# The even stage one half of the tokens at a time, and its narrow unit as one product of 448 columns

## The reference, cut to what matters

```
x = layer_norm(ALPHA * x + ffn, ln_ffn_g[layer], ln_ffn_b[layer])     # end of the first block
...
def modulate(x, shift, scale):
    return layer_norm_2(x) * (1 + scale[..., None, :]) + shift[..., None, :]
...
EVEN_IN_SIZES = (GLA_QK_W, GLA_QK_W, GLA_V_W, 2 * GLA_GATE_RANK, GLA_V_W,
                 MLA_Q_RANK, MLA_KV_RANK, MLA_ROPE, MLA_V_W)
proj = lambda h: split_cols(jnp.einsum('bnd,de->bne', h, w_in), EVEN_IN_SIZES)
gq_l, gk_l, gv_l, glr_l, gg_l, cq_l, ckv_l, kr_l, mg_l = proj(h_lat)
```

## Time and profile before

| | us |
|---|---|
| median of 3 runs (lowest, highest) | 1438.95 (1438.36, 1439.72) |
| the profiled execution | 1438.28 |
| its span, first to last instruction | 1437.0 |
| PE busy | 1109.3 (77%) |
| DVE busy | 465.4 (32%) |
| ACT busy | 323.1 (22%) |
| POOL busy | 87.9 (6%) |

### The profile page before, as it was taken

The page is one execution under the profiler, slowest core; times in us unless marked ns, Lnnn a source line. Parts: engine busy times, 40 slices in busy tenths (PEclk is TensorE's granted clock), DMA queues, the critical chain, the costliest instruction groups (busy, mean ns, idle before and its releaser), DMA issues.

```text
span 1437.0 us, 19484 instructions
## 1 busy us (share of the span) xinstructions
PE 1109.3 (77%) x8553; PEld 629.3 (44%) x8553; DVE 465.4 (32%) x943; ACT 323.1 (22%) x618; POOL 87.9 (6%) x116
## 2 busy tenths in 40 slices
PE   8999756698485656999985656666655799989998
PEld 7656312264131211897731211112111289744997
DVE  5636203101110100777720100100100077566774
ACT  4512110000310000374210000000000046433640
POOL 2311100000000000040120000000000000000100
PEclk9999978889788878999997888878787899999999
DMA  9949999999999999848999999999999964213720
GB/s 375 400 176 352 423 428 427 427 428 426 427 426 429 427 427 422 374 164 352 413 393 426 428 429 426 429 429 426 426 428 428 422 276 154 70 63 140 303 104 30
DMA packets 42699, 501.27 MB, mean 349 GB/s; under 512 B 6398, under 2 KB 7892, under 8 KB 13432
## 3 DMA queue, kind: packets, MB, share of 16 engines
q1 hardware_dynamic: 37440, 492.78, 82.0%
q10 hardware_dynamic: 3112, 5.96, 1.2%
q0 software_dynamic: 2064, 1.30, 0.3%
HBM read 498.92 MB, written 1.10 MB: 348 GB/s over the span
## 4 chain that ended last, share of the span: by engine, by line
DMA 44%; PE 39%; DVE 8%; ACT 5%; SPq 2%; issue 1%; POOL 1%; DVEq 0%; ACTq 0%; POOLq 0%
DMA weight_ring<-in_moe_w_gate_up 29%; DMA weight_ring<-in_u_down 11%; PE bank L1410 6%; PE bank L369 5%; PE bank L1440 3%; PE bank L370 3%; PE bank L372 3%; PE bank L371 3%; DMA weight_ring<-in_u_ctx_kv 2%; PE bank L632 2%; SPq L555 2%; DMA weight_ring<-in_u_last 2%; PE bank L1059 1%; PE bank L1853 1%; DVE weight_ring_rounded L410 1%
## 5 line engine op out<-in xcount | busy, mean ns | idle before, releaser
L1410 PE MATMUL bank<-weight_ring,expert_tokens 128*32 128x512 f32 x1952 | 290.7, 729 | 170.1 <-DMA weight_ring<-in_moe_w_gate_up 165.1
L1410 PEld LDWEIGHTS bank<-weight_ring,expert_tokens 128*32 128x32 f32 x1952 | 62.4, 122 | 371.3 <-DMA weight_ring<-in_moe_w_gate_up 211.0
L1440 PE MATMUL bank<-weight_ring,actT 128*32 128x256 f32 x1760 | 140.7, 478 | 60.0 <-DMA weight_ring<-in_u_down 51.7
L1644 DVE TENSOR_TENSOR act<-silu,bank 128x256 f32<-128x256 f32 x32 | 13.5, 420 | 399.1 <-ACT silu L1759 399.1
L1440 PEld LDWEIGHTS bank<-weight_ring,actT 128*32 128x32 f32 x1760 | 65.1, 132 | 126.5 <-DMA weight_ring<-in_u_down 55.6
L1759 ACT ACTIVATE silu<-bank 128x256 f32<-128x256 f32 x32 | 12.3, 384 | 452.4 <-PE bank L1410 452.4
L1658 DVE COPY expert_outs<-bank 32x256 f32<-32x256 f32 x60 | 25.1, 418 | 230.6 <-PE bank L1440 229.6
L410 DVE TENSOR_TENSOR weight_ring_rounded<-weight_ring,weight_ring_rounded 128x1024 fp32r<-128x1024 f32 (+1 forms) x76 | 89.3, 1235 | 14.3 <-ACT weight_ring_rounded L394 14.1
L394 ACT CAST weight_ring_rounded<-weight_ring 128x1024 fp32r<-128x1024 f32 (+1 forms) x72 | 70.0, 1046 | 19.5 <-DMA weight_ring<-in_u_qkv 8.8
L1776 ACT COPY expert_outs<-bank 32x256 f32<-32x256 f32 x60 | 21.9, 365 | 209.5 <-PE bank L1440 208.8
L524 POOL TENSOR_TENSOR norm_rstd<-norm_var,minus_half 128x1 f32<-128x1 f32 x12 | 12.1, 1008 | 844.2 <-DVE norm_var L1693 647.6
(11 more groups left out here) (523 smaller groups left out, 1849.7 us busy)
## 6 DMA issues: line engine op xcount, KB each, us to landing
weight_ring<-in_moe_w_gate_up SPq DMA_DIRECT2D x122, 2048.0 KB, 36.6
weight_ring<-in_u_down SPq DMA_DIRECT2D x55, 2048.0 KB, 37.1
weight_ring<-in_u_ada SPq DMA_DIRECT2D x9, 2048.0 KB, 7.8
weight_spare<-in_moe_w_gate_up SPq DMA_DIRECT2D x6, 2048.0 KB, 40.0
weight_spare<-in_u_down SPq DMA_DIRECT2D x5, 2048.0 KB, 41.1
weight_ring<-in_u_last SPq DMA_DIRECT2D x16, 512.0 KB, 32.6
...
```

Source lines behind the costliest of these rows:

```text
L1410: last = pe.matmul(up[CAP * j:CAP * (j + 1), :], B.xs[:, t, e * CAP:(e + 1) * CAP], w[:, t % 2, :, j, :], start=(t == 0), stop=(t == T - 1))
L1440: last = pe.matmul(K[3][CAP * q:CAP * (q + 1), 0:QC], B.actT[i][:, s, j * CAP:(j + 1) * CAP], w[:, jj, s, q, :], start=(j == 0 and s == 0) ...
```

## The change

Half 0 goes first. VectorE takes half 0's second moments right behind x of half 0, ahead of the norm of half 1 (second_moments_vector, called in experts_norm_vector), and hands the negated mean over; ScalarE only computes the result (first_flat_scalar). TensorE turns half 0, does 4 idle products, multiplies half 0's HIGH pass, turns half 1, and goes on with the passes of both halves. ScalarE modulates all 8 tiles of half 0, and tiles 4 to 7 of half 1, VectorE tiles 0 to 3 of half 1, each of 128 tokens. The narrow unit becomes two products of 448 columns with tokens in the partitions, n0 and n1, in one bank each. The low-rank rows then have tokens in the partitions too, so they are copied (low_rank_rows), turned by TensorE between the two column blocks of q, and copied again by ScalarE (job "lr", behind the first step of the latent attention) before the gate products. Banks keep their numbers for q and what follows. ScalarE rounds all four pieces of the narrow weights ahead of flat of half 0.

The diff, cut to its core:

```
--- before.py
+++ after.py
@@ -1712,6 +1712,8 @@
             x = B.x[:, half, :]
             v.scalar_tensor_tensor(x, x, B.rstd[:, half:half + 1], B.bias, ALU.mult, ALU.add).then_inc(*sig.tell("normed", ("x", stage, half)))
+            if half == 0 and stage == "moe1":
+                self.second_moments_vector("even", 0)
...
-    def modulated_tensor(self, stage, banks, between, block=None):
-        sig, pe, B = self.sig, self.pe, self.B
-        for c in range(2):
-            pe.wait_ge(*sig.after("summed", BEFORE[stage], 1, c))
-        for half in range(H):
...
-            pe.wait_ge(*sig.after("flat", stage, half))
-            for pair in range(T // 2):
-                for t in (2 * pair, 2 * pair + 1):
-                    o = (t % 2) * S + half * P
-                    last = pe.transpose(banks[pair][:, o:o + P], B.flat[:, half, t::T], B.ident)
-                if half == 1:
-                    last.then_inc(*sig.tell("tensor_turned", ("flat_turned", stage, pair)))
...
-    def modulated_vector(self, stage, banks, slot, hi, lo):
...
-        for pair in (0, 2):
-            v.wait_ge(*sig.after("flat_turned", stage, pair))
-            for t in (2 * pair, 2 * pair + 1):
-                v.tensor_scalar(lo[:, t, :], banks[pair][:, (t % 2) * S:(t % 2 + 1) * S], B.mod[:, slot, 1, t:t + 1],
-                                B.mod[:, slot, 0, t:t + 1], ALU.mult, ALU.add).then_inc(*sig.tell("modulated", ("modulated", stage, pair)))
-        for pair in range(T // 2):
-            both = slice(2 * pair, 2 * pair + 2)
-            v.wait_ge(*sig.after("h_rounded", stage, pair))
-            v.tensor_tensor(self.B.h_lo[stage][:, both, :], lo[:, both, :], hi[:, both, :], ALU.subtract).then_inc(
-                *sig.tell("h_split", ("features", stage, pair)))
...
-    def token_pass_tensor(self, stage, name, w, h, parts, half, bank):
+    def token_pass_tensor(self, stage, name, w, h, parts, half, bank, end=TOKENS_REST):
...
+    def second_moments_vector(self, stage, half):
+
+        sig, v, B = self.sig, self.v, self.B
+        stats, mv = (B.first_stats, B.first_mv) if half == 0 else (B.flat_stats, B.flat_mv)
+        v.wait_ge(*sig.after("x", BEFORE[stage], half))
+        for c in range(2):
+            v.bn_stats(stats[:, 6 * c:6 * c + 6], B.x[:, half, c * 512:(c + 1) * 512]).then_inc(*sig.tell("flat_moments"))
+        v.wait_ge(*sig.now("flat_moments"))
+        v.bn_aggr(mv, stats).then_inc(*sig.tell("flat_moments", ("flat_mean", stage, half)))
+        v.wait_ge(*sig.after("flat_mean", stage, half))
+        v.tensor_scalar(B.flat_var[:, half:half + 1], mv[:, 1:2], EPS_SECOND, None, ALU.add).then_inc(
+            *sig.tell("flat_variance", ("flat_variance", stage, half)))
+        if half == 0:
+            v.tensor_scalar(B.flat_sum[:, 0:1], mv[:, 0:1], -1.0, None, ALU.mult).then_inc(*sig.tell("flat_moments", ("flat_minus_mean", stage)))
...
+    def first_flat_scalar(self, stage):
+
+        sig, a, B = self.sig, self.a, self.B
+        minus_mean, bias = B.flat_sum[:, 0:1], B.flat_sum[:, 1:2]
+        a.wait_ge(*sig.after("flat_deviation", stage, 0))
+        a.wait_ge(*sig.after("flat_minus_mean", stage))
+        a.activation(bias, minus_mean, ACT.Copy, scale=B.flat_rstd[:, 0:1]).then_inc(*sig.tell("flat_steps"))
+        a.wait_ge(*sig.now("flat_steps"))
+        a.activation(B.flat[:, 0, :], B.x[:, 0, :], ACT.Identity, scale=B.flat_rstd[:, 0:1], bias=bias).then_inc(
+            *sig.tell("flat_steps", ("flat", stage, 0)))
...
-    def modulated_scalar(self, stage, banks, slot, hi, lo):
...
     EVEN_ORDER = {
...
-        "vector": ("cq", "ckr", "A", "+v", "L", "q", "A", "A", "+gg", "L", "L", "L", "v", "A", "A", "L", "+mg", "A", "A", "A"),
+        "vector": ("n1", "A", "+v", "L", "q", "A", "A", "+gg", "L", "L", "L", "v", "A", "A", "L", "+mg", "A", "A", "A"),
...
-    EVEN_JOBS = ("lr", "cq0", "cq1", "ckr0", "ckr1", "q", "k", "v0", "v1", "gg0", "gg2", "mg0", "mg2")
-    EVEN_BESIDE = ("gate0", "gate2", "lat", "cqT", "qr0", "qr1", "qrT0", "qrT1")
+    EVEN_BANKS = {"n0": 4, "n1": 5, "q": 3, "k": 4, "v0": 5, "v1": 0, "gg0": 1, "gg2": 2, "mg0": 3, "mg2": 4}
+    EVEN_AFTER = {"q": ("modulated", "even", 0, 1), "k": ("even_taken", "n0"), "v0": ("even_taken", "n1"), "v1": ("modulated", "even", 1, 0),
+                  "gg0": ("modulated", "even", 1, 1), "gg2": ("modulated", "even", 0, 0), "mg0": ("even_taken", "q"),
+                  "mg2": ("even_taken", "k")}
+    EVEN_BESIDE = ("lr", "gate0", "gate2", "lat", "cqT", "qr0", "qr1", "qrT0", "qrT1")
...
-        self.modulated_tensor("even", K, 0)
-        self.idle_products_tensor(K[5], 3)
...
+            if job == "q":
+                self.feature_pair("even", name, w, [c], h, self.even_bank(job))
+                self.low_rank_turned_tensor()
+                last = self.feature_pair("even", name, w, [c + P], h, self.even_bank(job)[:, S:2 * S])
+            else:
+                last = self.feature_pair("even", name, w, [c, c + P], h, self.even_bank(job))
...
+        banks = [self.even_bank(f"n{half}")[:, 0:w[0].shape[-1]] for half in range(H)]
+        run = lambda parts, half: self.token_pass_tensor("even", "even_narrow", w, h, parts, half, banks[half], self.WEIGHTS_REST)
+        self.halves_turned_tensor("even", 0)
+        self.idle_products_tensor(self.B.bank[5], 4)
+        run(self.HIGH, 0)
+        self.halves_turned_tensor("even", 1)
+        run(self.TOKENS_REST, 0)
+        run(self.HIGH, 1)
+        run(self.TOKENS_REST, 1)
+        for half in range(H):
+            run(self.WEIGHTS_REST, half).then_inc(
+                *sig.tell("projected", ("even", f"n{half}"), ("free", "even_narrow"), ("free", "even_narrow_hi")))
+
+    def low_rank_turned_tensor(self):
+
+        sig, pe, B = self.sig, self.pe, self.B
+        self.beside_free("lr")
+        for half in range(H):
+            pe.wait_ge(*sig.after("even_taken", f"lr{half}"))
+            last = pe.transpose(self.beside_bank("lr")[0:2 * GR, half * P:(half + 1) * P], B.lr_rows[:, half, :], B.ident)
+        last.then_inc(*sig.tell("side_products", ("beside", "lr")))
 
     def even_out(self):
...
+            buf, at = {"lr": (B.lr_rows, 0), "cq": (B.cq, 2 * GR), "ck": (B.ckr, 2 * GR + QR)}[job[0:2]]
+            dst = buf[:, int(job[-1]), :]
+            return dst, self.even_bank(f"n{job[-1]}")[:, at:at + dst.shape[-1]]
...
-        self.modulated_vector("even", K, 0, B.h_hi["even"], B.h_raw["even"])
+        self.second_norm_vector("even")
+        v.wait_ge(*sig.after("modulation", 0))
+        for q in range(2):
+            self.half_rest_vector("even", 0, q)
+        self.half_modulated_vector("even", 0, 1, range(4))
+        for q in range(2):
+            self.half_rest_vector("even", 1, q)
         self.split_weights_vector("even_narrow", T * sum(n for _, n in EVEN_W[0][1]))
         self.split_weights_vector("even_qk")
 
         def run(job):
-            for j in {"cq": ("cq1",), "ckr": ("ckr1",), "q": ("q",), "v": ("v1",)}.get(job, ()):
+            if job == "n1":
+                v.wait_ge(*sig.after("even", "n1"))
+                for j in ("lr1", "cq1", "ckr1"):
+                    v.tensor_copy(*self.even_take(j)).then_inc(*sig.tell("vector_moved", ("even_taken", j), ("even_taken", "n1")))
+                return
+            for j in {"q": ("q",), "v": ("v1",)}.get(job, ()):
...
-        self.split_weights_scalar("even_narrow", narrow, (0, 1))
-        self.flat_scalar("even")
-        self.split_weights_scalar("even_narrow", narrow, (2, 3))
-        self.modulated_scalar("even", K, 0, B.h_hi["even"], B.h_raw["even"])
+        self.split_weights_scalar("even_narrow", narrow)
+        self.first_flat_scalar("even")
+        a.wait_ge(*sig.after("modulation", 0))
+        for q in range(2):
+            self.half_modulated_scalar("even", 0, 0, range(4 * q, 4 * q + 4))
+            self.half_rounded_scalar("even", 0, q)
+        self.half_modulated_scalar("even", 0, 1, range(4, T))
+        for q in range(2):
+            self.half_rounded_scalar("even", 1, q)
...
+            if job == "n0":
+                a.wait_ge(*sig.after("even", "n0"))
+                for j in ("lr0", "cq0", "ckr0"):
+                    a.copy(*self.even_take(j)).then_inc(*sig.tell("scalar_moved", ("even_taken", j), ("even_taken", "n0")))
+                return
+            if job == "lr":
+                a.wait_ge(*sig.after("beside", "lr"))
+                a.copy(B.lrT[0:2 * GR, :], self.beside_bank("lr")[0:2 * GR, 0:S]).then_inc(*sig.tell("scalar_moved", ("beside_taken", "lr")))
+                return
...
-            pe.wait_ge(*sig.after("even_taken", "lr"))
+            pe.wait_ge(*sig.after("beside_taken", "lr"))
```

81 lines of the change are left out of this document (10 added, 71 removed), and 4 rows, old and new, of the table EVEN_ORDER.

## The result

The changed kernel takes 1441.17 us (median of 22 runs, 1439.39 to 1443.37); the kernel before, beside it, 1438.68 (22 runs, 1438.12 to 1440.05). The ratio is 1.0016, with a 95% interval of 1.001 to 1.0023: 2.5 us slower, within the 0.2% that the prediction called the same, 0.9 above its 1440.3 and inside its range. The profiled execution took 1441.83 us, its span 1440.3, against 1438.28 and 1437.0.

The account below looks back on a forecast made before the run. VectorE's queue was taken to bound the kernel through its copy of ckr: later splits and extra copies add 1.39 us, about 1.4 on the 1438.95 median, giving 1440.3 us; 8-in-10 range 1437.8 to 1442.8.

Parts of the forecast that it names:

- rival D: Narrow stage: TensorE's clock falls to 0.50 at about 1175, 4.2 us reach the path, 1444.5 us; chance 0.10.
- A: The forecast itself: VectorE's splits become the bound, 1440.3 us, own range 1439.2 to 1441.4; chance 0.69.
- The bound: Narrow stage: VectorE runs splits and three copies without a gap; TensorE's last narrow product ends 2 us before the copies.
- The start: First even transposes: flat half 0 ready at about 1165.4, but 40 idle products leave only 0.26 of 1.2 us.
- Half 0 to the second transposes: Even stage, timed from the odd stage: 5.14 + 1.01 - 0.11 us, so half 1's transposes start at 1172.5.
- The splits: VectorE's 8 weight pieces queue behind the last subtractions: start 1176.86 against 1173.12, end 3.74 us later at 1185.50.
- The sum: VectorE's copy of ckr starts at 1185.95 against 1184.56, +1.39 us, and all that follows is displaced by it.
- a small clock loss: Allowance for TensorE's clock within the 8-in-10 range, 1437.8 to 1442.8 us; no size of its own given.
- TensorE's head start is worth nothing: From 1184.56 to 1228 the moment of VectorE's ckr copy sets the time, so TensorE being ahead gains nothing.
- B: Even-stage modulations cost less than in the odd stage, by the page's figure 1.5 us less: 1438.8 us; chance 0.07.
- C: Narrow products saved come off in full, the splits not being waited for: 4.6 us less, 1434.4 us; chance 0.06.
- The covers: Half 1's moments (1.8 us later), the low-rank detour (5 us of cover) and the mla load would cost nothing.

Follow-up runs that it names:

- e3: The changed kernel with VectorE's four narrow splits moved into its idle gaps among the even stage's rests and modulations; 1438.3 us, ratio 0.9997.
- e6: e5 with 34 instead of 40 idle products ahead of the even transposes; 1439.36 us, ratio 1.0004.
- e5: The changed kernel with idle products in TensorE's narrow-stage gaps and ahead of the mg products; 1439.82 us, ratio 1.0004.
- e4: The change's 448-column products alone, both halves normed, turned and modulated together as in the kernel before; 1436.49 us, ratio 0.9986.
- e1: The changed kernel with idle products in TensorE's gaps of the narrow stage only; 1440.38 us, ratio 1.0011.
- e2: The changed kernel with 12 idle products ahead of the mg products only; 1439.81 us, ratio 1.001.
- r1: The changed kernel profiled again without any edit; 1442.21 us (one run).
- r2: The changed kernel profiled once more without any edit; 1440.57 us (one run).
- e10: e5 with each 448-column product cut into one of 288 and one of 160 columns; 1439.85 us, ratio 1.001.
- e9: e5 with half 0's moments back on ScalarE, its four narrow casts staying in front; 1440.48 us, ratio 1.0013.
- e8: e4 with 12 idle products ahead of mg and VectorE's three copies put ahead of its last qk split piece; 1435.31 us, ratio 0.9973.

## Why the prediction was right, and what was mis-sized

**The number.** The forecast was 1.4 us over the kernel before; measured are 2.5. That it came out within 0.9 of 1440.3 owes something to luck: one term was 0.4 too high, another, 1.35, was left out, and the three runs of the kernel before that it was added to had a median 0.27 above that of the 22. One of the prediction's own signs of being wrong came as well, the clock at 0.50 between 1170 and 1185, which it gave to rival D. So A was right as to what bounds the stage, and D's mechanism ran beside it at a smaller size.

**The bound: right.** VectorE's queue took over, with no idle time from the last subtraction to ckr and TensorE 2.2 us ahead (2 were foreseen). e3 shows it by moving nothing but that queue. But the times behind the first transposes came later than forecast: the second transposes at 1172.90 for 1172.5, the splits at 1177.96 for 1176.9, ckr at 1186.94 for 1186.0, and the rows of the chain behind it stand 2.4 and later 3.3 behind for 1.4.

**The start: right.** Flat half 0 was ready at 1164.12 + 1.24 = 1165.36 (ScalarE's last pass; 1165.4 forecast), and the idle products hid it (e6). T0 came 0.45 earlier and not 0.26: I took the modelled end of the last idle product (1157.29 + 9.09 = 1166.38) for its place in the queue, and the transposes start 0.16 ahead of that end, since records in a row overlap.

**Half 0 to the second transposes: right but for the clock.** 6.04 was forecast from the odd stage, 5.93 came in e5, 6.68 in the changed kernel. A 448-column product takes 0.203 (e4: 1176.70 to 1179.94, 16) to 0.218 (e5's halves), near the 0.199 taken.

**The splits.** Without a fall they start 3.43 later (e5, counted from the expert products), forecast 3.74. 3.43, less the 2.90 from the end of the splits to ckr before (1181.66 to 1184.56), plus 0.43 for two copies in front (0.55 forecast; the 32 columns take 0.10 from start to start, not 0.2), is 0.96, and the traces have 0.97. The sum had 1.39. This term was too high by 0.4.

**TensorE's clock: the term left out of the sum.** Of the 2.5 us, 1441.17 less e5's 1439.82, 1.35, is rival D's mechanism; the intervals of the two ratios just overlap, and the traces carry it: in the profiled execution it is 1.4 + 0.9 of 3.3. I had given it 0.10 and a price of 4.2, all of it beyond 2.2 us lost; the range took in "a small clock loss" without a figure. The idle stretches that I had foreseen, 1.2, 1.2 and 0.7 us, came as 1.05, 1.01 and 0.48. The price failed in three points. I let the fall begin at about 1175 and act on the 32 products left, behind which TensorE has slack; it began at 1171 and acted on the four products and eight transposes on which VectorE waits, where there is none, so that it counts from the first tenth. It ended 3.4 us later by itself, so it costs 1.4. And I looked for idle time only in the stage that was changed: the second fall lies 50 us on, where TensorE's lead becomes a wait of 3.02 us. "TensorE's head start is worth nothing" was too kind; it is worth less than nothing. How much of the 1.35 each fall has in the median stays open: e1 (first fill alone) gives 0.8, e2 (second alone) 1.36, together more than both fills give, each with an interval wider than their difference.

The Trainium skill, TensorE: Matmul & The Clock Gate, "HAM oscillation", tells that compute thinned out by waits throttles the engine again on every turn. The traces agree in kind (granted 0.50 behind the waits) but not in regularity: r1 fell and r2 did not, with the same waits. The page's case is a wait for transfers at every step; here TensorE waits for ScalarE and VectorE.

**B and C: wrong.** Four modulations of 128 columns take ScalarE 1.50, as in the earlier trace rows. The Trainium skill's figure for that (VectorE: DVE Perf Modes, "The TRN2 errata"), estimated at 0.25 us each, is not met: the trace has 0.375. The fixed extra latency that the prediction took from there is told of operations that read SBUF, while a modulation reads PSUM; only the figure bears on it. The prediction's reason, that most of a modulation is fixed, compared VectorE's 256 columns with ScalarE's 128; ScalarE alone bears it out: two of 256 take 0.91 from start to start before (1168.40 to 1169.31), 0.455 each, for half the columns 0.38. And e10 shows that saved products give nothing while VectorE is the bound.

**The covers held.** Half 1's moments, the low-rank detour and the mla load cost nothing: in e2, e5, e9 and e10 ckr to att is 53.16 to 53.18, before 53.19. One small thing I can't explain: what lies around the span is 1.52 us on average in the changed kernel's runs and 1.30 to 1.32 in those of the kernel before; it is 1.49 to 1.54 in all kernels with half 0's moments on VectorE and timed in several runs, 1.32 in e9, and 1.40 and 1.36 in e4 and e8. These 0.2 us are what is left of the 2.5 beside 0.97 and 1.35.
